# Cross-attention queries with the weights held in TensorE, in a two-part transformer on one core

## What is computed

```python
def memory_cross_attention(h, mem, wq, wkv, wo, mem_norm):
    B, S, _ = h.shape
    M = mem.shape[1]
    q = (h @ wq).reshape(B, S, H_X, DH_X)
    kv = (rms_norm_2(mem, mem_norm) @ wkv).reshape(B, M, 2, H_X, DH_X)
    s = jnp.einsum('bshd,bmhd->bhsm', q, kv[:, :, 0]).astype(jnp.float32) * (DH_X ** -0.5)
    p = jax.nn.softmax(s, axis=-1)
    o = jnp.einsum('bhsm,bmhd->bshd', p.astype(kv.dtype), kv[:, :, 1]).reshape(B, S, H_X * DH_X)
    return o @ wo
...
        h = rms_norm_2(x, g[2])
        y = memory_cross_attention(h, mem, xa_wq[l], xa_wkv[l], xa_wo[l], xa_mem_norm[l])
        x = x + rms_norm_2(y, g[3])
```

## Time and profile before

| | |
|---|---|
| median of 3 runs | 1357.84 us |
| lowest and highest | 1357.55 and 1358.16 us |
| the profiled execution | 1359.49 us |
| its span, first to last instruction | 1357.7 us |
| mean granted TensorE clock | 0.999 of full speed |
| VectorE busy | 979.1 us (72%), 1510 instructions |
| ScalarE busy | 738.3 us (54%), 1153 instructions |
| the two cross-attention stages | from about 857 to 881 us, and from 1150 to 1174 us |

### The profile page before, as it was taken

One profiled execution on the slowest core, in us unless ns is written; L12 is line 12 of the kernel. 1 busy time (PEld: TensorE's weight loads), 2 busy tenths in 40 slices (PEclk: granted clock), 3 DMA queues, 4 the chain that ended last, 5 costly groups with the idle time before them and its releaser, 6 DMA issues.

```text
span 1357.7 us, 19403 instructions
## 1 busy us (share of the span) xinstructions
PE 1343.6 (99%) x7451; PEld 1130.6 (83%) x7451; DVE 979.1 (72%) x1510; ACT 738.3 (54%) x1153; POOL 125.0 (9%) x113
## 2 busy tenths in 40 slices
PE   9999999999999999999999999999999999999998
PEld 6788888888888888888888877888888878888886
DVE  5657878777665767877778687886667887776665
ACT  4565545455454754545555675654445675654443
POOL 0000002111000000211110102220000001400000
PEclk9999999999999999999999999999999999999999
DMA  8844356555555434766655623458875525366552
GB/s 280 273 155 155 126 185 215 188 187 186 186 188 184 156 124 156 227 199 198 198 186 186 185 94 126 140 202 216 219 215 189 169 95 163 118 192 203 193 190 89
DMA packets 146577, 242.25 MB, mean 178 GB/s; under 512 B 4603, under 2 KB 91403, under 8 KB 146222
## 3 DMA queue, kind: packets, MB, share of 16 engines
q1 hardware_dynamic: 142498, 226.97, 51.3%
q0 software_dynamic: 3712, 13.77, 3.8%
q10 hardware_dynamic: 276, 0.27, 0.1%
HBM read 239.03 MB, written 1.97 MB: 178 GB/s over the span
## 4 chain that ended last, share of the span: by engine, by line
PE 95%; DVE 2%; ACT 1%; DMA 1%; issue 1%; POOL 0%; DVEq 0%; ACTq 0%; POOLq 0%; SPq 0%
PE ps L1205 19%; PE ps L1143 16%; PE ps L1149 16%; PE ps L1152 16%; PE ps L1212 10%; PE ps L1311 3%; PE ps L1437 2%; PE ps L1406 1%; PE ps L1388 1%; PE ps L2050 1%; DMA raw<-in_w_in 1%; PE ps L1250 1%; PE ps L1247 1%; PE ps L1253 1%; PE ps L1589 1%; PE ps L2060 1%
## 5 line engine op out<-in xcount | busy, mean ns | idle before, releaser
L2740 DVE TENSOR_TENSOR wlo<-raw,whi 128x1024 fp32r<-128x1024 f32 (+2 forms) x423 | 510.5, 1218 | 270.7 <-ACT whi L2172 269.9
L2172 ACT CAST whi<-raw 128x1024 fp32r<-128x1024 f32 (+1 forms) x431 | 444.3, 1041 | 339.4 <-PE ps L1212 188.6
L1205 PE MATMUL ps<-act,whi 128*128 128x512 f32 x1120 | 266.4, 390 | 0.0
L1205 PEld LDWEIGHTS ps<-act,whi 128*128 128x128 f32 x1120 | 208.4, 188 | 42.2
L1143 PE MATMUL ps<-whi,mhi 128*128 128x512 f32 (+2 forms) x688 | 235.9, 392 | 0.0
L1149 PE MATMUL ps<-wlo,mhi 128*128 128x512 f32 (+2 forms) x688 | 231.1, 385 | 0.0
L1152 PE MATMUL ps<-whi,mlo 128*128 128x512 f32 (+2 forms) x688 | 231.0, 385 | 0.0
L1152 PEld LDWEIGHTS ps<-whi,mlo 128*128 128x128 f32 x688 | 129.3, 188 | 26.4
L1149 PEld LDWEIGHTS ps<-wlo,mhi 128*128 128x128 f32 x688 | 129.3, 188 | 25.9 <-DVE wlo L2740 0.4
L1212 PEld LDWEIGHTS ps<-act,wlo 128*128 128x128 f32 x1120 | 143.6, 191 | 5.5
L1143 PEld LDWEIGHTS ps<-whi,mhi 128*128 128x128 f32 x688 | 125.7, 189 | 23.7 <-issue 2.6
(11 more groups left out here) (338 smaller groups left out, 1538.9 us busy)
## 6 DMA issues: line engine op xcount, KB each, us to landing
raw<-in_mlp_w SPq DMA_DIRECT2D x64, 1024.0 KB, 5.2
raw<-in_w_up SPq DMA_DIRECT2D x44, 1024.0 KB, 5.2
raw<-in_w_in SPq DMA_DIRECT2D x38, 1024.0 KB, 5.1
raw<-in_w_down SPq DMA_DIRECT2D x22, 1024.0 KB, 5.0
raw<-in_ev_w_in SPq DMA_DIRECT2D x10, 1024.0 KB, 5.1
raw<-in_w_out SPq DMA_DIRECT2D x8, 1024.0 KB, 5.1
raw<-in_xa_wkv SPq DMA_DIRECT2D x4, 1024.0 KB, 5.5
raw<-in_ev_w_out SPq DMA_DIRECT2D x4, 1024.0 KB, 5.2
```

The source lines that it names most:

```text
L1205: nc.tensor.matmul(ps[:, bank0 + f, :], of(whi, h)[:, k, f * P:f * P + P], act2[:, kx].rearrange("p i n -> p (i n)"), start=kx == 0, stop= ...
L2172: nc.scalar.copy(whi[:, m % HL, 0:w], raw[:, n % RAW, h * w:h * w + w]).then_inc(hi_done, 1)
L2740: nc.vector.tensor_tensor(wlo[:, m % HL, 0:w], raw[:, n % RAW, h * w:h * w + w], whi[:, m % HL, 0:w].bitcast(F32), ALU.subtract).then_inc( ...
```

## The change

Per layer of the second part:

- The query product holds the weights instead of the activations. For each block of the width it now takes the column halves f = 0 and 1 of wq, holds a 128 x 128 block of `whi` or `wlo`, and streams the 256 rows of `mhi` or `mlo` past it. Again 48 matmuls of 256 columns. Bank 6 then holds the queries of heads 0 and 1, for all rows, and bank 7 those of heads 2 and 3, with the head's columns on the partitions.
- So the query is not turned any more: the four transposes, the two evictions to `proj` and the plan's two groups are gone. ScalarE copies bank 6 straight to `qT[:, 0, :]`, times the score scale, and VectorE bank 7 to `qT[:, 1, :]`. No `rstd` is in `qT`, and no minus sign.
- The norm's factor now scales the exponent: exp(rstd * score + low), scale and bias both read from SBUF. `low` is the row maximum times minus `rstd`: a reduction by maximum, and a second small instruction of VectorE behind a wait on the first.
- On TensorE the key transposes stand ahead of the last quarter of the query product, and `scores(4)` waits for nothing of its own.

```diff
-                def query(tt, gs):
+                def query(gs):
...
-                        o = ps[:, 6 + tt, 0:SEQ]
-                        rows_ = slice(tt * P, tt * P + P)
-                        for k in (2 * g, 2 * g + 1):
-                            nc.tensor.matmul(o, mhi[:, k, rows_], wh[:, k % 4, :], start=k == 0, stop=False)
-                            m0 = nc.tensor.matmul(o, mhi[:, k, rows_], wl[:, k % 4, :], start=False, stop=False)
-                            m1 = nc.tensor.matmul(o, mlo[:, k, rows_], wh[:, k % 4, :], start=False, stop=k == KD - 1)
-                        if tt == 0:
-                            sxx["turn_to"](g + 2)
-                            if g == 3:
+                        for f in range(2):
+                            o = ps[:, 6 + f, 0:SEQ]
+                            cols_ = slice(f * P, f * P + P)
+                            for k in (2 * g, 2 * g + 1):
+                                nc.tensor.matmul(o, wh[:, k % 4, cols_], mhi[:, k, :], start=k == 0, stop=False)
+                                m0 = nc.tensor.matmul(o, wl[:, k % 4, cols_], mhi[:, k, :], start=False, stop=False)
+                                m1 = nc.tensor.matmul(o, wh[:, k % 4, cols_], mlo[:, k, :], start=False, stop=k == KD - 1)
+                            if f == 0 and g == 3:
                                 m1.then_inc(q_out, 1)
-                        elif g % 2:
+                        if g % 2:
                             m0.then_inc(pe_out, 1)
                             m1.then_inc(pe_out, 1)
-
-                def turn_query(tt):
-
-                    pe.wait_ge((q0_ready, q1_ready)[tt], l + 1)
-                    turn_blocks(("qkx", l, 1 + tt), [proj[:, tt, b * P:(b + 1) * P] for b in range(2)])
...
-                query(0, range(4))
+                query((0, 1, 2))
                 pe.wait_ge(ev_act, evs_act2(l, "k"))
                 turn_blocks(("qkx", l, 0), [kvn[:, tt, b * P:(b + 1) * P] for b in range(2) for tt in range(TT)])
-                query(1, (0, 1))
-                turn_query(0)
-                query(1, (2, 3))
+                query((3,))
                 pe.wait_ge(grp_dve, plan.by_number[plan.groups["qkx", l, 0]][2])
-                pe.wait_ge(grp_act, plan.by_number[plan.groups["qkx", l, 1]][1])
+                pe.wait_ge(q0_ready, l + 1)
...
                 scores(0)
+                pe.wait_ge(q1_ready, l + 1)
                 scores(2)
-                turn_query(1)
-                pe.wait_ge(grp_dve, plan.by_number[plan.groups["qkx", l, 2]][2])
                 scores(4)
...
+                act.wait_ge(q_out, l + 1)
+                nc.scalar.activation(qT[:, 0, :], ps[:, 6, 0:SEQ], ACT.Copy, scale=SCALE).then_inc(q0_ready, 1)
+                split_half(n0 + 14)
                 act.wait_ge(rstd_ready, rs_count["xx", l])
-                act.wait_ge(q_out, l + 1)
-                nc.scalar.activation(proj[:, 0, 0:256], ps[:, 6, 0:256], ACT.Copy, scale=rstd[:, NORM["xx", l], 0:1]).then_inc(q0_ready, 1)
-                key = ("qkx", l, 1)
-                group_ready(act, key)
-                nc.scalar.activation(qT[:, 0:2, 0:P], ps[:, bank_of(key), 0:SEQ].rearrange("p (b n) -> p b n", b=2), ACT.Copy,
-                                     scale=-SCALE).then_inc(grp_act, 1)
-                split_half(n0 + 14)
...
-                    nc.scalar.activation(step_of(1536, u, d), scores_of(u, d), ACT.Exp, scale=-1.0,
+                    nc.scalar.activation(step_of(1536, u, d), scores_of(u, d), ACT.Exp, scale=rstd[:, NORM["xx", l], d["qt"]:d["qt"] + 1],
                                          bias=low[:, d["qt"], s:s + 1], accum_out=den[:, d["qt"], s:s + 1]).then_inc(at_e, 1)
...
-                    nc.vector.tensor_reduce(low[:, d["qt"], d["slot"]:d["slot"] + 2], scores_pair(d), AX.X, ALU.min).then_inc(at_t, 2)
+                    at = low[:, d["qt"], d["slot"]:d["slot"] + 2]
+                    k = mark(nc.vector.tensor_reduce(at, scores_pair(d), AX.X, ALU.max))
+                    after(k)
+                    nc.vector.tensor_scalar(at, at, rstd[:, NORM["xx", l], d["qt"]:d["qt"] + 1], -1.0, ALU.mult, ALU.mult).then_inc(at_t, 2)
...
-                    dve.wait_ge(rstd_ready, rs_count["xx", l])
                     wait_turned(dve, plan.jobs["wq", l][0])
-                    nc.vector.tensor_scalar(proj[:, 1, 0:256], ps[:, 7, 0:256], rstd[:, NORM["xx", l], 1:2], None, ALU.mult).then_inc(q1_ready, 1)
+                    nc.vector.tensor_scalar(qT[:, 1, :], ps[:, 7, 0:SEQ], SCALE, None, ALU.mult).then_inc(q1_ready, 1)
...
-                query_turned()
                 lows(1)
```

More of the change, by code:

```diff
@@ L224, in build_network @@
         plan.group(("qkx", l, 0), "dve")
-        plan.group(("qkx", l, 1), "act")
-        plan.group(("qkx", l, 2), "dve")
         for tt in range(TT):
@@ L795, in bank_of @@
                 return 2
-            if key[0] == "qkx" and key[2] == 2:
-                return 5
             if key[0] == "ox":
@@ L1978, in query @@
                         m = 2 * n + g // 2
-                        if tt == 0:
-                            if g % 2 == 0:
-                                wait_lo(pe, m)
-                            sxx["need"](g)
+                        if g % 2 == 0:
+                            wait_lo(pe, m)
+                        sxx["need"](g)
                         wh, wl = (w[:, m % HL, :].rearrange("p (k n) -> p k n", k=KD // 2) for w in (whi, wlo))
-                        o = ps[:, 6 + tt, 0:SEQ]
-                        rows_ = slice(tt * P, tt * P + P)
-                        for k in (2 * g, 2 * g + 1):
-                            nc.tensor.matmul(o, mhi[:, k, rows_], wh[:, k % 4, :], start=k == 0, stop=False)
-                            m0 = nc.tensor.matmul(o, mhi[:, k, rows_], wl[:, k % 4, :], start=False, stop=False)
-                            m1 = nc.tensor.matmul(o, mlo[:, k, rows_], wh[:, k % 4, :], start=False, stop=k == KD - 1)
-                        if tt == 0:
-                            sxx["turn_to"](g + 2)
-                            if g == 3:
+                        for f in range(2):
[6 more added lines that the diff above has]
+                            if f == 0 and g == 3:
                                 m1.then_inc(q_out, 1)
-                        elif g % 2:
+                        if g % 2:
                             m0.then_inc(pe_out, 1)
                             m1.then_inc(pe_out, 1)
-                def turn_query(tt):
-                    pe.wait_ge((q0_ready, q1_ready)[tt], l + 1)
-                    turn_blocks(("qkx", l, 1 + tt), [proj[:, tt, b * P:(b + 1) * P] for b in range(2)])
                 def cross_out(tt, c):
@@ L3609, in query_out @@
                 def query_out():
-                    dve.wait_ge(rstd_ready, rs_count["xx", l])
                     wait_turned(dve, plan.jobs["wq", l][0])
-                    nc.vector.tensor_scalar(proj[:, 1, 0:256], ps[:, 7, 0:256], rstd[:, NORM["xx", l], 1:2], None, ALU.mult).then_inc(q1_ready, 1)
-                def query_turned():
-                    key = ("qkx", l, 2)
-                    group_ready(dve, key)
-                    nc.vector.tensor_scalar(qT[:, 0:2, P:SEQ], group_bank(key)[:, 0:SEQ].rearrange("p (b n) -> p b n", b=2), -SCALE, None,
-                                            ALU.mult).then_inc(grp_dve, 1)
+                    nc.vector.tensor_scalar(qT[:, 1, :], ps[:, 7, 0:SEQ], SCALE, None, ALU.mult).then_inc(q1_ready, 1)
                 def weights_out(tt):
@@ L3679, in _ @@
                 query_out()
+                dve.wait_ge(rstd_ready, rs_count["xx", l])
                 lows(0)
-                query_turned()
                 lows(1)
```

## The result

The changed kernel takes 1364.66 us (median of 6 runs, 1363.27 to 1365.21). The kernel before, run beside it, takes 1357.65 (6 runs, 1357.24 to 1358.16). The ratio is 1.0051, with a 95% interval of 1.0042 to 1.0061: **7.0 us or 0.5% slower**. The prediction was 1358.0, no measurable change, with a range to 1359.0, so it was wrong.

A forecast was written before the change was run, and what follows sets the result against it. The prediction took TensorE, busy in 99% of the span, as the bound. Terms of -0.22, +0.21 and +0.07 us made +0.06 per layer, +0.12 for both; 1357.84 + 0.1 gave 1358.0 us, range 1357.1 to 1359.0.

The forecast's parts named there:

- Term 2: Maxima on VectorE: the new small multiplication behind each reduction adds 0.21 us before the first exponent.
- Rival 3: TensorE's granted clock falls from 2.4 to 1.2 GHz behind an idle piece of about 0.7 us: +6 us per layer; chance 0.015.
- Term 1: Query products up to the first scores: two transposes leave TensorE's chain, -0.22 us.
- the query products: 48 per layer before and after, same columns and 0.12 us spacing; holding weights instead of activations gains or loses nothing.
- The first eviction: ScalarE's copy of the finished query half into qT takes 0.385 us, hidden by 0.2 us before the first scores.
- Term 3: Exponents with a second SBUF operand, 0.09 us longer and 0.56 apart, make TensorE 0.05 to 0.07 us late from the first values.
- Where the stall goes: TensorE's 0.52 us hole before the third scores becomes the exponents' transposes waiting for ScalarE, 0.6 to 0.8 us per stage.
- Sum: Whole change: -0.22 + 0.21 + 0.07 = +0.06 us per layer, +0.12 for both.

The follow-up runs named there:

- first run: The changed kernel with the row maxima written to unused PSUM columns and read there by the small multiplication: 1357.76 us, ratio 1.0005 to the kernel before.
- seventh run: The changed kernel with the plain minimum straight into the exponents' bias and no small multiplication: 1357.27 us, ratio 0.9998.
- third run: The changed kernel with eight unused matmuls of 512 columns between the third scores and the first transposes of the exponents: 1362.51 us, ratio 1.0041.
- runs eight and ten: The changed kernel with maxima in every second element of a small buffer (1363.9 us); with the multiplication as two SCALAR_TENSOR_TENSOR of 128x1 (1365.98 us).
- fifth run: The kernel with maxima left in PSUM and multiplied from there, with the exponent's scale as constant 1.0 instead of the norm factor: 1357.36 us, ratio 0.9998.
- second experiment: The changed kernel with GpSimd starting its two subtractions of the stage only after the fourth maxima: 1371.49 us, ratio 1.0107.
- runs eight to ten: The changed kernel with the small multiplication on every second element (1363.9 us), as one SCALAR_TENSOR_TENSOR of 128x2 (1363.41) or two of 128x1 (1365.98).
- repaired kernels: The changed kernel with the small multiplication reading maxima from PSUM (1357.76 us), or split into two instructions of 128x1 (1357.83 us).

## Why the prediction was wrong

Slower by more than 0.2% had a chance of 0.025 on record, and none of the rivals was a wait of VectorE for GpSimd. By its own steps:

- **Term 2, the maxima (+0.21 us): this step failed.** I priced the small multiplication by the pair in the earlier trace rows, 0.04 + 0.17 us. At 820.60 GpSimd was idle; at 863.38 it was in the middle of two subtractions, a row that I had in the earlier trace rows and used only to ask when ScalarE's cast was needed. The term held no wait for GpSimd at all, and that wait is what made the loss. Without that neighbour my figure is nearly right: 0.10 us of gap and 0.22 (first run) make 0.32 instead of 0.21, and the seventh run against the first puts it at 0.35 of the stage (22.88 against 22.53). With it, the first pair waits 1.1 us and the second 1.4. Compare the stage of 25.20 (third run, clock 1.00) with 22.88: **2.3 us per stage, 4.6 in all.** The trace of before held the warning. The same line L3519, a small operation with two inputs in SBUF, appears twice in VectorE's timeline, and GpSimd's row stands beside the long one:

```profile
1109.33 0.16 DVE L3519 TENSOR_TENSOR rden<-den,small 128x16 f32<-128x16 f32 x1
1119.78 0.92 DVE L3519 TENSOR_TENSOR rden<-den,small 128x16 f32<-128x16 f32 x1
```

```profile
1119.37 1.30 POOL L1063 TENSOR_TENSOR mlo<-o_nat,mhi 128x512 fp32r<-128x512 f32 x1 [0.81 <-ACT mhi L2556]
```

  Both end within 0.03 us of each other, at 1120.7. A group's spread of durations (160 to 917 ns here) is the question to ask of any row that is to price a new instruction.
- **Rival 3, the clock (chance 0.015): the mechanism came true, by another cause than its hole of 0.7 us.** The hole was 1.71 us and the clock fell behind it, for 1.17 us in a stage of the changed kernel and for 1.6 to 1.9 us in the stages of runs eight and ten (26.8 to 27.1 against 25.2), instead of 6 per layer. Its argument against, that 1.99 us at the start did no harm, did not carry over: that hole came between products of 512 columns with no other hole close behind it, this one after the scores with a second hole of 0.64 close behind. Which of these matters was not tried.
- **Term 1 (-0.22) and the query products: right.** From the first query product to the first scores it was 6.49 us before (857.75 to 864.24) and is 6.28 after (855.46 to 861.74), so -0.21. With Term 3 the forecast for a kernel without the small operation is -0.15 per stage, and the seventh run shows -0.06.
- **The first eviction: right.** It took 0.386 us and was hidden, and no wait for ScalarE stands before the first scores.
- **Term 3 (+0.05 to 0.07): right in kind, a little small.** The exponents took 560 ns and stood 0.55 apart, and the fifth run makes 0.11 us per stage of it. The rule that each pointer operand adds about 93 ns, from the page "ScalarE: Activation LUTs" of the Trainium skill, section What ACT_TABLE_LOAD costs, holds for the second operand too: 563 less 473 is 90 ns.
- **Where the stall goes: right in place, wrong in size.** The 0.52 before the third scores went, and a wait of the exponents' transposes for ScalarE took its place. In the changed kernel it is 1.71 us; without the wait for GpSimd, in the first run, it is 0.64, within the 0.6 to 0.8 foretold.
- **Sum.** Of 7.0 us, 0.6 are the change's ordinary cost (0.29 per stage, first run; forecast 0.06), 4.6 the wait for GpSimd and 2.1 the clock. Together 7.3, which is 0.3 too much. The three come from different sources (stages of profiles and medians of runs), and the clock's share is the loosest of them.

## What to carry to other kernels

Before a small VectorE instruction is put on a path, look at what GpSimd does in that moment, not only at VectorE and at the one that waits. If GpSimd runs something long, an operation of 0.2 us can take as long as GpSimd's instruction has left; with the operand read from PSUM, or with one element per instruction and one tensor input, it did not here. Price a new instruction from a row with the same neighbours, and ask of any group whose shortest and longest durations lie far apart what ran beside the long one. And whoever moves a step on a queue should first list what stands behind it, as the second experiment shows at a price of 14 us.

## What the runs showed of the hardware that was not expected

- Two instructions of 128x1 (0.33 us together) are 1.0 us faster than one of 128x2 (1.30) while GpSimd subtracts.
- Two numbers per partition are enough for the wait, and with two inputs in SBUF a single one is (1.60 of 1.67 us).
- The granted clock fell behind a hole of 1.71 us in one stage of the changed kernel and stayed at 1.00 behind the same hole in the other (26.36 and 25.19 us). Of the three other forms with that hole (runs eight to ten), two had it fall in both stages, to 0.50 in a stretch, and one in one stage. Behind 1.99 us at the start of the kernel before it did not fall. What decides this stays open. Eight products in the hole kept the clock at 1.00.
- Why the repaired kernels are not better than before by all that was removed is known in part: a wait for the first exponents stands in TensorE's way, 0.64 us in the first run and still 0.34 in the seventh, and no run took it away.
